# Input projections of a hybrid recurrent decoder step: one fp32 matmul or three fp32r products per weight block

## What is computed

```
z = rms(x) @ w_in                       # one projection, columns shared by all mixers
o_hg, o_rw, o_gl, o_ml = hgrn2(z), rwkv7(z), gla(z), mlstm(z)   # recurrences, 4 heads of 64
gates = sigmoid(z_gate)                 # 4 x 1024 columns
mix = sum_n gates[n] * (o_n @ w_branch[n])
x = x + mix @ w_out
x = x + relu(rms(x) @ w_up) ** 2 @ w_down
y = rms(x)
```

## Time and profile before

| what | value |
|---|---|
| median of 3 runs | 2544.01 us (2543.95 to 2546.87) |
| the profiled execution, its own time | 2548.29 us |
| its span in the trace | 2546.6 us |
| busy PE / DVE / ACT / POOL | 93% / 40% / 21% / 11% of the span |
| mean granted clock of TensorE | 0.964 of full speed |
| mLSTM projections, first fills (to the first mLSTM tile) | 0 to 224.7 us |
| mLSTM tiles, last tile | 224.7 to 384.6, to 437.7 us |
| GLA projections | 437.7 to 500.9 us |
| GLA tiles, last tile | 500.9 to 849.9, to 928.9 us |
| RWKV preparation | 928.9 to 1079.5 us |
| RWKV tiles, last tile and last fills | 1079.5 to 1401.4, to 1504.1 us |
| branches, output projection, MLP | to 2546.6 us |

### The profile page before, as it was taken

How to read it: one execution, slowest core, us unless ns; L and a number is a source line. 1 busy time by engine, 2 the same in 40 slices (tenths; PEclk the granted TensorE clock), 3 DMA queues, 4 the chain that set the end, 5 groups by cost and what they waited for, 6 DMA issues and landing times.

```text
span 2546.6 us, 31679 instructions
## 1 busy us (share of the span) xinstructions
PE 2369.5 (93%) x12565; PEld 1951.2 (77%) x12565; DVE 1028.0 (40%) x1593; ACT 532.3 (21%) x718; POOL 285.4 (11%) x383
## 2 busy tenths in 40 slices
PE   6999999999999887799999879999999997999995
PEld 3697555566666654487878659999999997999995
DVE  1031232355555334633333326663222224555554
ACT  2211110412112102311111023201101003333342
POOL 1000000321313020000000017421000001000012
PEclk9999998999999978899999899999999998999998
DMA  3112112611111141101010146413111124111111
GB/s 141 38 36 70 51 51 55 205 51 51 51 36 54 46 130 35 51 18 35 17 34 17 35 130 214 145 41 114 47 41 49 59 85 181 42 41 44 47 41 77
DMA packets 46749, 172.05 MB, mean 68 GB/s; under 512 B 6128, under 2 KB 6464, under 8 KB 46432
## 3 DMA queue, kind: packets, MB, share of 16 engines
q1 hardware_dynamic: 23040, 85.72, 11.0%
q0 software_dynamic: 15840, 55.59, 6.6%
q10 hardware_dynamic: 7808, 29.87, 2.9%
HBM read 126.27 MB, written 44.88 MB: 67 GB/s over the span
## 4 chain that ended last, share of the span: by engine, by line
PE 74%; issue 13%; DVE 4%; POOL 4%; DMA 2%; ACT 1%; POOLq 0%; DVEq 0%; SPq 0%; ACTq 0%
PE PS L615 19%; PE PS L437 16%; PE PS L1267 15%; PE PS L1228 4%; PE PS L433 3%; PE PS L411 2%; PE PS L1150 2%; PE PS L1138 2%; PE PS L1146 2%; POOL AR L758 1%; PE PS L498 1%; POOL AR L756 1%; PE PS L528 1%; PE PS L862 1%; PE PS L1104 1%
## 5 line engine op out<-in xcount | busy, mean ns | idle before, releaser
L437 PE MATMUL PS<-HT,RING 128*128 128x358 f32 x2400 | 782.3, 473 | 25.1 <-ACT CF L457 14.2
L437 PEld LDWEIGHTS PS<-HT,RING 128*128 128x128 f32 x2400 | 449.5, 192 | 272.8 <-issue 24.3
L1267 PE MATMUL PS<-ACT_parts,CF_parts 128*128 128x358 f32 x1152 | 319.6, 331 | 24.8 <-DVE ACT_parts L593 14.0
L615 PE MATMUL PS<-HT_parts,CF_parts 128*128 128x358 f32 x768 | 251.7, 328 | 0.9 <-ACT AR L567 0.9
L615 PE MATMUL PS<-OT_parts,CF_parts 128*128 128x358 f32 x768 | 251.2, 327 | 0.0
L615 PE MATMUL PS<-HT_parts,RING_parts 128*128 128x358 f32 x768 | 250.8, 327 | 0.0
L1267 PE MATMUL PS<-ACT_parts,RING_parts 128*128 128x358 f32 x768 | 250.5, 326 | 0.0
L1267 PEld LDWEIGHTS PS<-ACT_parts,CF_parts 128*128 128x128 f32 x1152 | 207.1, 189 | 34.0 <-issue 28.6
L457 ACT ACTIVATE OT<-PS 128x358 f32<-128x358 f32 x108 | 50.6, 469 | 522.2 <-PE PS L437 516.6
L1600 ACT ACTIVATE ACT_parts<-AR 128x1074 fp32r<-128x1074 f32 x96 | 105.8, 1103 | 193.7 <-PE PS L1267 179.1
L615 PEld LDWEIGHTS PS<-HT_parts,CF_parts 128*128 128x128 f32 x768 | 144.6, 188 | 1.3 <-ACT AR L567 1.2
(11 more groups left out here) (374 smaller groups left out, 3343.9 us busy)
## 6 DMA issues: line engine op xcount, KB each, us to landing
RING<-in_w_all SPq DMA_DIRECT2D x132, 512.0 KB, 3.3
AR<-gates POOLq DMA_DIRECT2D x32, 537.0 KB, 3.9
proj<-OT ACTq DMA_DIRECT2D x18, 537.0 KB, 5.1
gates<-OT ACTq DMA_DIRECT2D x18, 537.0 KB, 5.1
AR<-proj POOLq DMA_DIRECT2D x14, 537.0 KB, 10.4
gates<-CF ACTq DMA_DIRECT2D x14, 537.0 KB, 5.2
AR<-in_xT SPq DMA_DIRECT2D x8, 537.0 KB, 13.2
AR<-in_xT POOLq DMA_DIRECT2D x8, 537.0 KB, 7.3
```

What stands on the lines that cost most here:

```text
L437: last = e.matmul(PS(6 + c % 2, 0, GRP), RING[:, u, k, :], HT[:, k, g * GRP:(g + 1) * GRP], start=k == 0, stop=k == KD - 1)
L615: last = e.matmul(PS(3 * u + g, 0, GRP), a_[:, u, k, :], b_[:, k, t], start=k == 0 and i == 0, stop=k == KD - 1 and i == 2)
L1267: last = e.matmul(PS(3 * v + g, 0, GRP), a_[:, u, 4 * v + r % 4, :], b_[b][:, t], start=r == 0 and i == 0, stop=r == 31 and i == 2)
```

## The change

Every step of the input projection becomes three fp32r products (`three`): with the weights split into a rounded high part and the rest, and the normalised activations likewise, it adds high by high, high by low and low by high. In detail:

- The activations' parts (HT_R, OT_R) are made once, in the prologue, by ACT (high) and DVE (low).
- A chunk's high part is made by ACT: `weight_hi`, a copy of 128x1024 into WHIA_R. In the fills it stands in `fill_out` right behind the second eviction of the *other* chunk: after c = 1 for slot 1 of the same pair, after c = 4 for slot 0 of the next.
- The low part is made by POOL in place: `weight_lo`, a subtraction of 128x1024. PE waits for it (`split0`, `split1`) where it waited for the load.
- mLSTM's and GLA's values were projected by token; now they go channel-major like everything else. They are transposed on PE: 18 transposes once for mLSTM, 4 at the head of each GLA tile from a buffer that POOL fills for each tile (`load_v`, 256 KB in pieces of 512 bytes; GVR, GVT).
- Memory is re-laid: outputs of the first two mixers are stored to DRAM (`MIXED`) ahead of barriers 2 and 3 and loaded back before the branches (six loads); the states of the decode rows are loaded later; ACT joins barrier 2 before it evicts the first groups behind it.
- The prologue adds squares in pairs on DVE (4 PE rounds for 8), and interleaves the small projection with the first chunk.

```diff
+        def weight_hi(e, u, p):
+
+            e.wait_ge(S(f"chunk_loaded{u}"), (p + 1) * 16)
+            e.activation(WHIA_R[:, u], RING[:, u], ACT.Copy).then_inc(S("weights_hi"), 1)
+
+        def weight_lo(e, u, p):
+
+            e.wait_ge(S("weights_hi"), p * 2 + (u + 1))
+            e.tensor_tensor(RING_R[:, u], RING[:, u], WHIA_R[:, u].bitcast(F32), ALU.subtract).then_inc(S(f"split{u}"), 1)
+
+        def three(e, out, u, k, t, first, end):
+
+            for i, (a_, b_) in enumerate(((WHIA_R, HT_R), (WHIA_R, OT_R), (RING_R, HT_R))):
+                last = e.matmul(out, a_[:, u, k, :], b_[:, k, t], start=first and i == 0, stop=end and i == 2)
             return last
...
+        def pe_chunk(e, u, p, ev):
+
+            e.wait_ge(S(f"split{u}"), p + 1)
+            e.wait_ge(S(f"banks_free{u}"), ev + 1)
+            for k in range(KD):
+                for g in range(3):
+                    last = three(e, PS(3 * u + g, 0, GRP), u, k, slice(g * GRP, (g + 1) * GRP), k == 0, k == KD - 1)
+            last.then_inc(S(f"chunk_done{u}"), 1)
+
+        def fill_work(e, q):
...
-                    e.wait_ge(S(f"chunk_loaded{u}"), (q + (P_FILL + 1)) * 16)
+                    e.wait_ge(S(f"split{u}"), q + (P_FILL + 1))
                 e.wait_ge(S("fill_free"), q * 6 + (c + 1))
-                if by_token:
-                    for t in range(4 * g, min(4 * g + 4, TILES + 1)):
-                        w = P if t < TILES else LASTW
-                        for k in range(KD):
-                            last = e.matmul(PS(6 + c % 2, (t % 4) * P, (t % 4) * P + P)[0:w], HT[:, k, t * P:t * P + w],
-                                            RING[:, u, k, :], start=k == 0, stop=k == KD - 1)
-                else:
-                    for k in range(KD):
-                        last = e.matmul(PS(6 + c % 2, 0, GRP), RING[:, u, k, :], HT[:, k, g * GRP:(g + 1) * GRP],
-                                        start=k == 0, stop=k == KD - 1)
-                        if k < KD - 1:
-                            yield
+                for k in range(KD):
+                    last = three(e, PS(6 + c % 2, 0, GRP), u, k, slice(g * GRP, (g + 1) * GRP), k == 0, k == KD - 1)
+                    if k < KD - 1:
+                        yield
                 last.then_inc(S("fill_done"), 1)
...
+            row = stage[u]
+            e.activation(row[:, g * GRP:(g + 1) * GRP], PS(6 + c % 2, 0, GRP), ACT.Copy).then_inc(S("fill_free"), 1)
+            if c == 1:
+                weight_hi(e, 1, q + P_FILL)
+            if c == 4 and not last:
+                weight_hi(e, 0, q + (P_FILL + 1))
...
-            with e.Fori(0, TILES) as n:
+            def gl_tile(n):
+                weight_lo(e, 1, n + (P_FILL + Q_GL_TILES))
                 gl_by_head(n, P, HALVES)
+                weight_lo(e, 0, n + (P_FILL + Q_GL_TILES + 1))
+                e.wait_ge(S("gl_vt"), n + 1)
+                load_v(n + 1)
...
+            e.wait_ge(S("gl_out"), TILES)
+            save_mixed(slice(0, TILES * P))
+            weight_lo(e, 0, P_FILL + Q_RW_PRE)
             e.wait_ge(S("states_final"), 2)
             gl_states(True)
-            e.wait_ge(S("out"), 22 * 16)
+            weight_lo(e, 1, P_FILL + Q_RW_PRE)
+            e.wait_ge(S("gl_out"), TILES + 1)
+            save_mixed(slice(TILES * P, W))
+            e.wait_ge(S("out"), (16 + 12) * 16)
             barrier(e, 3)
...
+            e.wait_ge(S("fill_done"), Q_END * 6)
+            for k in (0, 1, 4, 5, 6, 7):
+                e.dma_start(OT[:, k], MIXED[k]).then_inc(S("ot_back"), 16)
...
-            rms_pe(e, 0)
-
-            e.wait_ge(S("ws"), 16)
+            rms_pe(e)
+
+            e.wait_ge(S("ws"), 32)
+            e.wait_ge(S("split0"), P_ML + 1)
             for k in range(KD):
                 e.wait_ge(S("ht_ready"), k + 1)
                 for g in range(3):
-                    last = e.matmul(PS(3 + g, 0, GRP)[0:68], WS[:, k, :], HT[:, k, g * GRP:(g + 1) * GRP],
+                    last = e.matmul(PS(3 + g, 0, GRP)[0:68], WS[:, k, :], XT[:, k, g * GRP:(g + 1) * GRP],
                                     start=k == 0, stop=k == KD - 1)
-            last.then_inc(S("small"), 1)
-            barrier(e, 1)
-
-            for p in range(2):
-                pe_pair(e, P_ML + p, P_ML + p)
-            pe_vpair(e, P_ML + 2, P_ML + 2)
-
-            fill = fill_work(e, 0, True)
-            steps(fill, 3)
+                if k == KD - 1:
+                    last.then_inc(S("small"), 1)
+                e.wait_ge(S("ot_ready"), k + 1)
+                for g in range(3):
+                    last = three(e, PS(g, 0, GRP), 0, k, slice(g * GRP, (g + 1) * GRP), k == 0, k == KD - 1)
+            last.then_inc(S("chunk_done0"), 1)
+            arrive(e)
+
+            pe_chunk(e, 1, P_ML, P_ML)
+            for p in range(P_ML + 1, P_FILL):
+                for u in range(2):
+                    pe_chunk(e, u, p, p)
+
+            fill = fill_work(e, 0)
+            steps(fill, 8)
...
+                v = GVT[0:w]
                 att = GATT.rearrange("p h t -> p (h t)")[0:w, 0:8 * w]
+                e.wait_ge(S("rows3"), n * 16 + 16)
+                for j in range(4):
+                    last = e.transpose(PS(0, j * P, j * P + P)[0:w], GVR[:, j, 0:w], ident)
+                last.then_inc(S("gl_vt"), 1)
                 steps(gate, 16)
...
             ml_tile(TILES, LASTW, True, outs)
             steps(outs, 6)
+            for u in range(2):
+                e.wait_ge(S(f"fill_sent{u}"), Q_RW * 16)
             arrive(e)
+            join(e, 2)
             fill_outs(e, Q_RW, range(0, 3))
-            join(e, 2)
...
+                e.wait_ge(S("gl_vt"), n + 1)
+                e.activation(GVT[0:w], PS(0)[0:w], ACT.Copy).then_inc(S("gl_v"), 1)
+                steps(outs, 1)
                 e.wait_ge(S("gl_x"), 2 * n + 1)
                 e.activation(x[:, :, 1:nl, :], x[:, :, 1:nl, :], ACT.Exp).then_inc(S("gl_e"), 1)
                 e.wait_ge(S("gl_x"), 2 * n + 2)
                 e.activation(x[:, :, 0:nl + 1:nl, :], x[:, :, 0:nl + 1:nl, :], ACT.Exp).then_inc(S("gl_e"), 1)
                 e.activation(x[:, :, nl + 1, :], tile_of(GK), ACT.Copy)
                 e.activation(q[:, :, 1, :], tile_of(GQ), ACT.Copy).then_inc(S("gl_dk"), 1)
-                steps(outs, 3 if last_tile else 4)
+                steps(outs, 2 if last_tile else 3)
```

More of the change, by code:

```diff
@@ L316, in build @@
         RE = a.take(g=2, t=W)
[L317 to L318 removed]
+        RTMP1 = a.at
         RCS = a.take(g=2, t=TILES)
@@ L388, in build, with mixed @@
         xs, ys = A["xT"], OUT["yT"]
[L389 to L393 removed]
+        PROJ = nc.dram_tensor("proj", (22, P, W), F32, kind="Internal").ap()
+        MIXED = nc.dram_tensor("mixed", (KD, P, W), F32, kind="Internal").ap()
+        STAGE_M = [STAGE_ML[:, u] for u in range(2)]
+        VT = M4[:, 2:4]
+        STAGE_GR = [ZS, STAGE_AR]
+        def mixed(k):
+            return OTR[:, k - 2] if k in (2, 3) else OT[:, k]
         block = ctx.enter_context(nc.Block())
@@ L487, in steps @@
                 next(work, None)
-        def pe_vpair(e, p, ev):
-            for u in range(2):
-                e.wait_ge(S(f"chunk_loaded{u}"), (p + 1) * 16)
-                e.wait_ge(S(f"banks_free{u}"), ev + 1)
-                for t in range(TILES + 1):
-                    w = P if t < TILES else LASTW
-                    o = 3 * u * 512 + t * P
-                    for k in range(KD):
-                        last = e.matmul(PSt[0:w, o:o + P], HT[:, k, t * P:t * P + w], RING[:, u, k, :],
-                                        start=k == 0, stop=k == KD - 1)
-                last.then_inc(S(f"chunk_done{u}"), 1)
         def evac(e, u, p, emit, copy_in=None):
@@ L571, in exp_ln_table @@
             e.preload_act_table_set("natural_log_exp_and_others")
-        def rms_dve(e, r, rst, src, dst, name, each=None):
-            e.wait_ge(S("rstd"), r + 1)
-            for k in range(KD):
-                ins = e.scalar_tensor_tensor(dst[:, k, :], src[:, k, :], col(name, k), rst, ALU.mult, ALU.mult)
-                if each is not None:
-                    each(ins)
-            return ins
-        rms_sq = [SQB]
         def split_hi(e, hi, x):
@@ L714, in pool_program @@
                         RM[:, NP:NT].rearrange("p (q c) -> p q c", q=NSEQ)[:, :, DSEQ - 1]).then_inc(S("out"), 16)
-            e.wait_ge(S("out"), 14 * 16)
+            e.wait_ge(S("ml_pre"), TILES + 2)
+            for g in range(2):
+                e.dma_start(MIXED[6 + g], OTM[:, g]).then_inc(S("out"), 16)
+            e.wait_ge(S("out"), 16 * 16)
             barrier(e, 2)
@@ L883, in _ @@
             last.then_inc(S("ml_mt"), 1)
-            steps(fill, 24)
-            steps(fill_work(e, 1, True), 24)
+            steps(fill, 48)
+            steps(fill_work(e, 1), 48)
             e.wait_ge(S("ml_go"), 2)
@@ L1011, in gl_tile @@
                         qs = GQX[:, g, s, :] if last_tile else q[:, g, 0, 0:w]
```

(4 more changed lines are left out.)

487 lines of the change are left out of this document (272 added, 215 removed).

## The result

The changed kernel took **2618.18 us** (median of 4 runs, 2616.31 to 2624.05) against 2543.98 us: a ratio of 1.0293, 95% interval 1.0275 to 1.0311. It is slower by 74 us, outside the range given. The span of the profiled execution is 2616.3 us against 2546.6, the mean granted clock 0.926 against 0.964.

What follows compares the result with a forecast made beforehand. PE was taken to set the pace in the tiles, an ACT and DVE chain in the RWKV preparation. Terms -41 -16 -7 +52 +3 +8 -16 -11 +7 sum to -21 us: median 2523 us, range 2470 to 2567.

Steps and rivals of the forecast that it cites:

- mLSTM tiles: mLSTM tiles: -16 us (0 to -22); 24 steps save 2.8 us per tile, against a wait of 0.8.
- The price of a step: Input projection: three fp32r products of 0.168 us each, 0.505 us per step instead of 0.622, saving 0.117.
- RWKV tiles: RWKV tiles: -16 us (-8 to -18); 18 of 24 steps save 2.1 us, six give nothing.
- GLA tiles, +52: GLA tiles: +52 us (+15 to +75), the deciding term; 50.1 us per tile with the clock, against 43.60.
- The two waits: GLA tile: PE waits 6.2 us ahead of the first level and 2.4 for the next tile's values.
- The rule: Rival, chance 0.06: low parts block DVE for whole POOL instructions at mLSTM and RWKV tile ends, +27, 2550 us.
- row 9's 0.4: Earlier trace: DVE's L1849 takes 0.77 us beside POOL's levels, 0.34 without; read as slowed by 0.4.
- Projections, -41: mLSTM projections: -41 us (-33 to -48), from cheaper chunks, squares in pairs and a barrier gone.
- the prediction's own signs of being wrong: Level 1 ending before PE's 16 steps, GLA tile under 45 or over 53 us, PE waiting for `split` in mLSTM projections.
- Barrier 2, -7: Last mLSTM tile and GLA projections: -7 us (-17 to +3); steps save 17, waiting costs about 10 with the clock.
- RWKV preparation, +8: RWKV preparation: +8 us (0 to +15); barrier 3 about 15 us after the tile's end, step blocks return 6.
- The low-clock rival (2567): GLA tiles: clock stays low 18 us, not 5.8, after the 6.2 us wait; +44, 2567 us, chance 0.18.

Runs made afterwards that it cites:

- e1_values: Changed kernel with the next GLA tile's value load issued ahead of slot 0's low part instead of behind it: 2571.43 us.
- e2_exps: Changed kernel with ACT's exponentials of a GLA tile ahead of the eviction of group 0 again, as before the change: 2599.74 us.
- e3_first: Changed kernel with the high part taken behind the other chunk's first eviction instead of its second, everywhere: 2532.93 us.
- e5_stages: Changed kernel with POOL's order moved outside GLA tiles: two low parts ahead of the convolution's stores, barrier 2's behind state stores, barrier 3's behind saved rows: 2602.64 us.
- e10_nostore: Changed kernel without storing the first two mixers' rows ahead of barriers 2 and 3; the branches load rows of the projections instead: 2606.94 us.
- e8_frozen: Changed kernel with three products per step but no later parts made; all chunks use the first two chunks' high parts: 2490.08 us.
- e7_single: Changed kernel's memory and orders, but one fp32 matmul per step with whole weights and no parts of weights made: 2594.1 us.

## Why the prediction was wrong

On the profiled spans the sum was -21 and the result +69.7 us, 91 apart. 33 of these are in the GLA tiles, and that term alone turns the sign. Another 48 are in four smaller terms that erred the same way: projections 13, mLSTM tiles 13, barrier 2 14.5, RWKV preparation 7.5. The rest is in the last fills and ahead of the branches. Its own steps:

- **The price of a step held.** Products come 0.165 us apart; the RWKV tiles gave 15.5 of 16 us (12 to 16 in the later runs with three products), the last GLA tile cost 3.8 rather than 3.
- **GLA tiles, +52, measured +84.7: the term that failed.** The two waits and their order were right, but the price of the low part beside DVE was wrong (next point), and so were the clock's and the load's. To the first level I had 14.3 us and it took 17.86: 2.0 is the clock, low in the 16 steps behind the wait for the values, where I charged a loss only once per tile; 1.9 is the low part, 4.19 us rather than 2.3; level 1 itself was 0.3 shorter. From there to the next tile I had 35.8 with the clock and it took 36.65: the values were 4.1 us late, not 2.4, and the rest of the stretch was some 0.8 shorter. Their issue takes 0.79 us on POOL, which I left out, and from its end to L1015 it is 3.85 us where I took 3.3. e1_values and e2_exps measure the two waits apart (-47 and -18), e3_first both with one edit (-85).
- **The rule was right, my reading of the earlier trace rows wrong.** I took 0.77 beside 0.34 us as "about half" of a block, where a whole block fits: the instruction of 0.77 us began 0.17 us into a POOL instruction of 0.73 us and ended 0.21 us after it, as L1932 ended 0.21 us after its low part. The Trainium skill (SBUF — State Buffer, section "Who interferes with whom") has the loser blocked for the whole instruction and lets issue order decide who that is. Three measurements agree: L1840 from 0.17 to 1.69 us, until the low part's end; L1932 from 0.35 to 2.53 where POOL began first; the low part from 2.42 to 4.19 where DVE began first. So row 9's 0.4 was what remained of a short POOL instruction. The Trainium skill's other half, for an instruction with at most one input in SBUF, agrees as well: L1838, with one input in PSUM, ran in 0.16 us beside a low part. In the mLSTM tiles this is the wait of 1.78 where I had 0.8, 8 of the 13 us missed there; e3_first, which removes it, is 9 us faster in that stage, and the other 5 were not taken apart. As a rival I had given the rule 0.06 and looked for it only at the tiles' ends, where the RWKV tiles then did not show it; its larger cost was in the GLA tile, the other way round, on POOL.
- **Projections, -41, measured -27.8.** 10.12 us of wait before the mLSTM tiles, as a low part stands behind stores, their landing and loads on POOL, and 6.0 in the prologue, where L897 waits for the first low part. Neither was in the sum, though POOL's order in the kernel shows both. PE waiting for a part in this stage was one of the prediction's own signs of being wrong, as was a GLA tile over 53 us.
- **Barrier 2, -7, measured +7.5.** PE waits 16.0 us, not 6.5: I had the stores behind the low part as 3 us, but before they had been issued from 427.59, 10 us ahead of the end of PE's tiles, and now all of them queue behind a low part that waits for a high part, and are issued from 401 us on, where PE's tiles end. e5_stages gives 7 us of this wait back, and e10_nostore, without the rows' own stores, 4.3.
- **RWKV preparation, +8, measured +15.5.** L1117 waits 41.86 us, against 16.45 in the earlier trace rows. I had barrier 3 about 15 us after the tile's end and it came 22.4 after it. The low part ended 12 us after the tile's end, which leaves 3 of my 15 for the stores; they took 1.5 us to issue, and POOL then stood 8.9 us at the barrier. That is the whole miss: from POOL's way out of the barrier to the first product 43.9 us pass, and 44.7 passed before (930.25 to 974.96). Without the stores (e10_nostore) POOL leaves this barrier 6.8 us sooner, with its low part behind them (e5_stages) 6.5; the product comes 4.3 and 4.8 sooner, and why not all of it comes through is open. With no parts made the product comes 12 us sooner (e8_frozen).
- **The low-clock rival (2567) was the nearest in time and had the wrong reason.** It needed more than 12 us at the low clock behind the wait ahead of level 1; PE worked 4.4 us at 0.50 behind that wait, and 5.9 behind the wait for the values. It is two waits per tile with a loss behind each that cost, not a long loss behind one.
- **One cost was in no rival.** In e7_single and e8_frozen, with no parts of weights at all, PE waits for DVE at level 3; the exponentials' new place is the likely cause. In the changed kernel this wait is hidden behind the larger one at level 1; e3_first uncovers it.

How much of e3_first's -85 is each wait's own was not tried apart, nor was e8_frozen with the exponentials ahead.
